# Attention of a hybrid backbone in two parts: the first latent tile ahead of the other three

## The reference

```python
h = x * (1 + scale1) + shift1                       # one combined input projection h @ w_in
o_rec = hgrn2_branch(...)                           # 8 heads, gated linear recurrence, both directions
o_att = attend(q, k, v)                             # 16 query heads of 64, 4 key heads, 640 keys for latent tokens
y = sigmoid(ga) * (o_rec @ w_branch_rec) + sigmoid(gb) * (o_att @ w_branch_att)
x = layer_norm(ALPHA * x + g1 * (y @ w_out))
h2 = x * (1 + scale2) + shift2
# PEER mixer: 8 heads, two top-16 lists of 128 keys each, then the top 16 of 16*16 sums
s = einsum(h2 @ w_query, sub_keys); s_top, i_top = top_k(s, 16)
best_s, best_pos = top_k(s_top[0][:, None] + s_top[1][None, :], 16); gate = softmax(best_s)
a = gelu(einsum(h2, u_tab[expert]))                 # 128 experts for each token, a row of 1024 each
x = layer_norm(ALPHA * x + g2 * einsum(gate * a, v_tab[expert]))
```

## Time and profile before

| what | value |
|---|---|
| median of 3 runs | 5783.16 us (5782.72 to 5789.52) |
| the profiled execution | 5785.87 us, span 5783.8 us |
| PE busy | 4596.6 us (79%) |
| DVE busy | 3766.0 us (65%) |
| POOL busy | 2196.6 us (38%) |
| ACT busy | 1375.0 us (24%) |
| moved by DMA | 1705.85 MB, mean 295 GB/s |

### The profile page before, as it was taken

One profiled execution on the slowest core, in us unless ns is written; L12 is line 12 of the kernel. 1 busy time (PEld: TensorE's weight loads), 2 busy tenths in 40 slices (PEclk: granted clock), 3 DMA queues, 4 the chain that ended last, 5 costly groups with the idle time before them and its releaser, 6 DMA issues. The chain is left out here.

```text
span 5783.8 us, 60711 instructions
## 1 busy us (share of the span) xinstructions
PE 4596.6 (79%) x17704; PEld 2562.3 (44%) x17704; DVE 3766.0 (65%) x7088; ACT 1375.0 (24%) x3576; POOL 2196.6 (38%) x1826
## 2 busy tenths in 40 slices
PE   7889988876856877777788999988778678777776
PEld 6556655644523332222265566556454343222222
DVE  2356778767788776754533477787677887667545
ACT  2112212310001333333321122122110013333333
POOL 0001124442656444455400011344416564444554
PEclk9899998888978999999999999978889789999999
DMA  6743345685979999999967433456959899999998
GB/s 262 264 179 104 120 150 206 209 334 219 354 295 377 381 421 420 416 421 416 398 220 269 148 113 125 177 188 205 347 198 377 303 349 392 421 421 415 420 415 346
DMA packets 296660, 1705.85 MB, mean 295 GB/s; under 512 B 33424, under 2 KB 43280, under 8 KB 176272
## 3 DMA queue, kind: packets, MB, share of 16 engines
q0 software_dynamic: 258048, 1342.29, 59.6%
q1 hardware_dynamic: 23712, 338.18, 15.4%
q10 hardware_dynamic: 14576, 21.52, 1.0%
HBM read 1696.61 MB, written 5.24 MB: 294 GB/s over the span
## 5 line engine op out<-in xcount | busy, mean ns | idle before, releaser
L366 POOL DMA_INDIRECT arena<-in_peer_uv,eidx x1024 | 1179.5, 1152 | 1642.3 <-POOLq L365 1402.0
L2148 DVE SCALAR_TENSOR_TENSOR arena<-arena 128x1024 f32<-128x1024 f32 x384 | 470.6, 1225 | 353.8 <-DMA arena<-in_peer_uv,eidx 342.7
L409 POOL DMA_INDIRECT arena<-in_peer_uv,eidx x384 | 504.0, 1313 | 477.8 <-POOLq L408 455.0
L864 PE MATMUL banks<-arena 128*128 128x512 f32 x896 | 493.3, 633 | 234.8 <-PEq L1476 231.5
L837 PE MATMUL banks<-ring,arena 128*128 128x512 f32 x864 | 386.7, 603 | 115.9 <-PEq L819 115.1
L866 PE MATMUL banks<-arena 128*128 128x512 f32 x896 | 469.8, 606 | 0.0
L461 ACT ACTIVATE arena<-arena 128x1 f32<-128x1 f32 (+1 forms) x772 | 156.9, 203 | 1044.7 <-ACTq L460 1044.5
L864 PEld LDWEIGHTS banks<-arena 128*128 128x128 f32 x896 | 151.5, 194 | 546.7 <-issue 546.4
L466 ACT ACTIVATE arena<-ident,arena 128x128 f32<-128x128 f32 x832 | 333.6, 401 | 238.3 <-ACTq L465 235.8
L2148 DVE SCALAR_TENSOR_TENSOR ring<-ring,arena 128x1024 f32<-128x1024 f32 x192 | 235.3, 1226 | 216.6 <-DMA ring<-in_peer_uv,eidx 214.3
L1879 DVE SCALAR_TENSOR_TENSOR arena<-arena 128x1024 f32<-128x1024 f32 x256 | 328.3, 1282 | 67.4 <-DMA arena<-in_peer_uv,eidx 50.7
(11 more groups left out here) (303 smaller groups left out, 7858.6 us busy)
## 6 DMA issues: line engine op xcount, KB each, us to landing
ring<-in_wblk SPq DMA_DIRECT2D x160, 2048.0 KB
arena<-in_peer_uv,eidx POOLq DMA_INDIRECT x1408
arena<-in_lnrows ACTq DMA_DIRECT2D x6, 1024.0 KB, 10.3
arena<-in_sk ACTq DMA_DIRECT2D x4, 1024.0 KB, 8.2
hT<-in_peer_uv,eidx POOLq DMA_INDIRECT x192
ring<-in_peer_uv,eidx POOLq DMA_INDIRECT x192
x<-in_x_sample ACTq DMA_DIRECT2D x1, 2048.0 KB, 28.9
out<-arena ACTq DMA_DIRECT2D x4, 512.0 KB, 7.3
```

The source lines that it names most:

```text
L366: nc.gpsimd.indirect_dma_start(grow[j], None, ins["peer_uv"], bass.IndirectOffsetOnAxis(ap=eidx[:, n, r:r + 1].bitcast(U32), axis=0)).then ...
L409: nc.gpsimd.indirect_dma_start(gslot[j], None, ins["peer_uv"].rearrange("(e h) d -> e (h d)", h=2), bass.IndirectOffsetOnAxis(ap=eidx[:, n ...
L864: nc.tensor.matmul(banks[:, b, :], diag[n], row[:, 0:CB], start=start, stop=stop, skip_group_check=True).then_inc(diag_used, 1)
L2148: V.scalar_tensor_tensor(u, u, 1.0, h2[:, t - 2, :], ALU.mult, ALU.mult, accum_out=av[:, r:r + 1])
```

## The change

Attention is split in two. First come two groups of eight units that hold all 16 heads of tile 1 (`LONE`, `members`), then tile 1's mixing, norm, queries and scores, then eight groups of six units for tiles 2 to 4. Tile 1's selection leaves `one_mix` and becomes 16 parts (`select_block`), one after each of the first 16 units of the second attention; from the 18th unit on two dots of tile 1 follow each unit, 60 in all. The mixing steps of tiles 2 to 4 then take 15 rows each (68 dots, then sums), and the rest of the 96 sums comes where all of them were.

Tile 0's rows move forward: 24 dots ahead of the first recurrence head (`GATE_ROWS`), 13 in each head, 44 sums among the norms, 32 in the first attention, 52 in tile 1's mixing (10 of them behind it). Tile 1's buffers now lie where row slots 4 to 7 are, so from sum 76 on tile 0's rows use four slots (`NARROW`), and tile 1's rows from the fifth on wait for the end of its selection (`slots_open`). The gelu of tile 0 moves to the start of the key stage.

Tiles 2 to 4 get buffers of their own (`grp_tile`), with a second load of the norm rows and sub-keys and a second spread of the modulation rows (`gains_in`, `fold_gains`). The selection of tile 2 starts by blocks as its scores come, and gives its row numbers in two halves (`joined_ids`). The second norm of tile 0 is finished between tile 2's rows. The queries are transposed straight from `qkv`, without POOL's copy.

```diff
-HEAD_ROWS = 6
-NORM_ROWS = 24
+GATE_ROWS = 24
+HEAD_ROWS = 13
+NORM_ROWS = 44
 UNIT_ROWS = 2
+NARROW = 76
+ONE_UNIT = 18
+ONE_EXP = 20
+ONE_ROWS = 2
+MIX_ROWS = 15
+
+
+def members(g):
+
+    if g < LONE:
+        return [(4 * g + n, 1) for n in range(4)]
+    return [(g - LONE, t) for t in range(2, NT)]
+
+
+def units_of(g):
+
+    return 2 * len(members(g))
...
 
+        def row_slot(part, r):
+
+            return r % 4 if part == 1 and r >= NARROW else r % ROWS
...
+        one_jobs = ONE_ROWS * (2 * GT * PAIRS - ONE_UNIT)
+        gelu_mix = (SLOTS - one_jobs + MIX_ROWS - 1) // MIX_ROWS + 1
+        assert one_jobs <= SLOTS and gelu_mix < KD
...
+                n, first, last = part % 2, 0, SLOTS
                 for r in range(first, last):
-                    j = r % ROWS
+                    j = row_slot(part, r)
                     if n == 0 and r % (SLOTS // 2) == 0:
                         stage_rows(r)
+                    if part == 2 and r == 4:
+                        pool.wait_ge(slots_open, 1)
+                        pool.sem_inc(slots_open, -1)
...
             for l in range(DEPTH):
-                ahead = dots_end + ROWS
-                single_rows(0, 0, min(ahead, SLOTS))
-                for p in range(PAIRS):
-                    if p in (0, PAIRS // 2):
-                        pool.wait_ge(qkn_pool, 1)
-                        pool.sem_inc(qkn_pool, -1)
-                    stage_queries(p)
-                    if p:
-                        for r in range(ahead, ahead + UNIT_ROWS * UNITS):
-                            if r < 2 * SLOTS:
-                                single_rows(r // SLOTS, r % SLOTS, r % SLOTS + 1)
-                        ahead += UNIT_ROWS * UNITS
-                for r in range(ahead, 2 * SLOTS):
-                    single_rows(r // SLOTS, r % SLOTS, r % SLOTS + 1)
-                single_rows(0, 0, SLOTS)
-                single_rows(1, 0, SLOTS)
+                for part in range(4):
+                    single_rows(part)
                 for t in range(2, NT):
                     n = t % 2
...
+                        if r in ((0, SLOTS // 2) if t == 2 else (0,)):
+                            c = slice(r, r + SLOTS // 2 if t == 2 else SLOTS)
+                            pool.wait_ge(idx_ready, 1)
+                            pool.sem_inc(idx_ready, -1)
+                            nc.gpsimd.tensor_copy(eidx[:, n, c].bitcast(U32), eid[:, 0, c].bitcast(U32)
+                                                  ).then_inc(idx_staged, 1)
+                            pool.wait_ge(idx_staged, 1)
+                            pool.sem_inc(idx_staged, -1)
+                            if c.stop == SLOTS:
+                                pool.sem_inc(idx_taken, 1)
...
 
+                gelu(0, SLOTS).then_inc(gelu_ready, 1)
                 act.dma_start(kpast, ins["cache_k"][l:l + 1].rearrange("a p n -> p (a n)")).then_inc(past_full, 16)
...
+                def attention(first, last):
+                    for b in (0, 2, 6):
+                        claim_pair(b)
+                    queries(first)
+                    claim(4)
+                    pe.sem_inc(bank_free[4], 1)
+                    for u in range(2):
+                        score(first, u)
+                    for g in range(first, last):
+                        att_group(g, g == first, g < last - 1)
+                    weigh(last - 1, units_of(last - 1) - 1)
+                    output(last - 1)
+                    for b in (0, 2, 6):
+                        pe.sem_inc(bank_free[b], 1)
+
+                attention(0, LONE)
                 phase_barrier(pe, "pe")
-
-
                 one_first = len(CTX_BLOCKS + LAT_BLOCKS)
                 one_mix(one_tile, one_first)
+                attention(LONE, GROUPS)
+                phase_barrier(pe, "pe")
+
+
                 grp_first = one_first + len(ONE_BLOCKS)
...
+                def joined_ids(half):
+
+                    c = slice(half * SLOTS // 2, (half + 1) * SLOTS // 2)
+                    V.scalar_tensor_tensor(e1[:, c], e1[:, c], float(NKEYS), e2[:, c], ALU.mult, ALU.add)
+                    dve.drain()
+                    if half == 0:
+                        dve.wait_ge(idx_taken, 1)
+                        dve.sem_inc(idx_taken, -1)
+                    V.tensor_scalar(eid[:, 0, c].bitcast(U32), e1[:, c], layer_base[:], None, ALU.add
+                                    ).then_inc(idx_ready, 1)
+
...
-                            ctx_rows((2 * SLOTS - jobs["at"] + 3 - n) // (4 - n))
+                            ctx_rows((2 * SLOTS - jobs["at"] + 4 - n) // (5 - n))
+                    fold_gains(tl)
...
+                def select_block(tl, n, part):
+
+                    if part == 0:
                         if n < 2:
                             dve.wait_ge(stage_ready, 1)
                             dve.sem_inc(stage_ready, -1)
-                        first_level(tl, tl.stage, 4 * n, 4 * n + 4)
+                        first_level(tl, tl.stage, 4 * n, 4 * n + 2)
+                    if part == 1:
+                        first_level(tl, tl.stage, 4 * n + 2, 4 * n + 4)
+                    if part == 2:
                         candidates(tl, 2 * n, 2 * n + 2)
                         second_level(tl, 2 * n, 2 * n + 2)
+                    if part == 3:
                         positions(gates[0], 2 * n, 2 * n + 2)
                         look_up_both(tl, 2 * n)
                         if n == 1:
                             dve.wait_ge(stage_ready, 2)
                             dve.sem_inc(stage_ready, -2)
                             one_ids(0)
+                        if n == 3:
+                            one_ids(1)
...
+                ctx_rows(GATE_ROWS)
+                softmax(gates[0])
...
+                def att_group(g, first, more):
+                    n = units_of(g)
+                    for u in range(n):
                         if u % 2:
                             arrived(4)
                             V.tensor_copy(PT[1], r3(pair(4, KEYS), P)).then_inc(bank_free[4], 1)
                             dve.drain().then_inc(pt_ready[1], 1)
-                        if u + 2 < UNITS:
-                            lowest(b, u + 2)
+                        if u + 2 < n:
+                            lowest(g, u + 2)
                         elif more:
-                            lowest(1 - b, u + 2 - UNITS)
-                        if u == 0 and p:
-                            normalise(1 - b)
-                        if u < 7 and p == 0:
-                            head_norm(512, 8, P, u)
-                        if u == 6 and p == 0:
-                            dve.drain().then_inc(qkn_pool, 1)
-                        ctx_rows(rows_at_unit(p, u))
-
-                for u in range(2):
-                    lowest(0, u)
-                for p in range(PAIRS):
-                    att_pair(p)
-                normalise(1)
+                            lowest(g + 1, u + 2 - n)
+                        if u == 0 and not first:
+                            normalise(g - 1)
+                        if g == 0 and u < 2:
+                            for part in ((2, 3), (4, 5, 6))[u]:
+                                head_norm(512, 8, P, part)
+                            if u == 1:
+                                dve.drain().then_inc(qn_ready, 1)
+                        if g < LONE:
+                            ctx_rows(UNIT_ROWS)
+                        else:
+                            at = (g - LONE) * n + u
+                            if at < 16:
+                                select_block(one_tile, at // 4, at % 4)
+                                if at == 15:
+                                    dve.drain().then_inc(slots_open, 1)
+                            if at >= ONE_UNIT:
+                                one_dots(ONE_ROWS * (at - ONE_UNIT), ONE_ROWS * (at - ONE_UNIT + 1))
+                            if at == ONE_EXP + 3:
+                                softmax(gates[0])
+
+                def attention(first, last):
+                    for u in range(2):
+                        lowest(first, u)
+                    for g in range(first, last):
+                        att_group(g, g == first, g < last - 1)
+                    normalise(last - 1)
+
+                for part in range(2):
+                    head_norm(512, 8, P, part)
+                attention(0, LONE)
                 phase_barrier(dve, "dve")
                 one_mix(one_tile)
+                ctx_rows(2 * SLOTS - jobs["at"])
+                dve.wait_ge(g2_ready, 1)
+                dve.sem_inc(g2_ready, -1)
+                second_norm(0, acc, bc2c, None, 0)
+                attention(LONE, GROUPS)
+                phase_barrier(dve, "dve")
 
...
-                mix(0)
-                for n in range(1, KD):
+                own = {"at": one_jobs}
+                for n in range(KD):
                     mix(n)
```

(66 more changed lines are left out.)

360 lines of the change are left out of this document (161 added, 199 removed).

## The result

The changed kernel took 5857.94 us (median of 4 runs, 5849.4 to 5865.5), the kernel before 5782.94 in the same comparison: a ratio of 1.0127, 95% interval 1.011 to 1.0145. It is slower by 75 us, where I forecast a gain of 58. The time lies outside my range and has the other sign.

A forecast was written before the change was run, and what follows sets the result against it. No engine bound the whole kernel; each stage had its own bound (DVE and PE in the heads, DMA in mixing). The terms summed to -29 us a layer, -58 in both: 5725 against the median of 5783.16, range 5635 to 5805.

The forecast's parts named there:

- The heads: Recurrence heads: seven more dots lie inside the chain of levels, 8.05 us a head, +64 us a layer.
- The lead-in: Ahead of the heads: 24 dots fit into DVE's wait and PE's wait mostly goes, -5 us a layer (0 to -9).
- The key stage: Key stage: sums, norms, gelu and waits take 94 us against 69, +25 a layer, bounds +15 and +32.
- Attention: Both attention parts: 99 and 245 us, together 344 against 317, +27 a layer, bounds +15 and +45.
- Tile 1's mixing: Tile 1's mixing and what follows: fewer rows, -32, and less behind it, -16; together -48 us a layer, bounds -70 and -15.
- Four slots: Rival in tile 1's mixing: four slots are too few, a row costs about 3 us, -48 becomes -11, 5799 us; chance 0.12.
- The sign that I had named: Tile 1's mixing: if no shorter than 132 us to its last row, the prediction is wrong.
- The mixing of tiles 2 to 4: Mixing of tiles 2 to 4: DVE is free when it begins, DMA is next in line, -50 us a layer, bounds -60 and -35.
- The end: From the last mixing step to tile 2's rows: PE's 44.92 us wait goes, -42 us a layer, bounds -50 and -25.
- The clock in the heads: Rival in the heads: PE pauses, its clock falls to 1.2 GHz, some 264 us a layer beyond the +64; chance 0.10.
- The heads hide their rows: Rival in the heads: DVE's idle time hides the dots, +20 for +64 a layer, 5637 us; chance 0.10.
- the end wins nothing: Rival ahead of tile 2's rows: query blocks starve the 51 sums, so these rows start no sooner, 5809 us; chance 0.08.

The follow-up runs named there:

- the four-slot run: The kernel before with tile 0's rows going through four slots, not eight, from sum 68 on, nothing else moved: 5863.62 us, ratio 1.0136.
- two of its versions: The kernel before, unedited (5782.94 us), and with 24 dots while gates are made and five of six dots a head behind its levels (5710.25 us).
- its last version: The changed kernel with eight rows before each mixing, five dots a head behind the levels and two under ACT's square root: 5631.58 us, ratio 0.9743.

## Why the prediction was wrong, step by step

- **The heads** (+64): right, with the mechanism. Seven dots are 8.05 us a head; with the lead-in it was +65. The level is 5.00 us long in the trace (592.52 to 597.52), 4.9 was forecast. The lead-in won nothing (-5): the first head starts on DVE at 458 in both kernels, since the last of the 24 dots ends at 456.3, where the softmax had stood. DVE did ten dots without a pause and then waited for the eleventh row:

```profile
438.46 1.23 DVE L1911 SCALAR_TENSOR_TENSOR arena<-arena 128x1024 f32<-128x1024 f32 x1 [6.76 <-DMA arena<-in_peer_uv,eidx]
```

Of the 16 issues that I had priced at the slow or the fast rate, four took 1.98 to 1.99 us, all beside dots without a gap between them, and ten 0.93 to 0.98 us: five while DVE waited, five beside dots that stood about 0.1 us apart. So the slow rate that my rule from the Trainium skill ("SBUF — State Buffer", Who interferes with whom) gave for all 16 held for a quarter of them. Two of the four lie on the way of the eleventh row, some 2 of the 6.76 us by this estimate; the rest is the way of the rows themselves, and from 438.4 on they came at 407 GB/s with DMA full.
- **The key stage** (+25): +33. The sums, the norms and the gelu were priced well. DVE stood 5.28 us ahead of the gelu's first reader, but 3.45 us stood at this place before, where the engines meet (`phase_barrier`); from PE's start behind the barrier (892.41) to the first sum (895.97) it was 3.6 us, and I had given 3. What I had too low were the waits: those for rows came to 7.4 us for 4 to 5, and 3 us stand at the norms, for which I had no term. The changed kernel, and then the kernel before:

```profile
894.17 0.29 DVE L1906 TENSOR_TENSOR arena<-arena 128x128 f32<-128x128 f32 x1 [5.28 <-DVEq L1905]
```

```profile
827.31 1.23 DVE L1876 SCALAR_TENSOR_TENSOR arena<-arena 128x1024 f32<-128x1024 f32 x1 [3.45 <-DVEq L295]
```

- **Attention** (+27): +29. 97 and 249 us for 99 and 245; selection in the units was priced rightly. One thing I had not reckoned with: PE took 266.6 us for the matmuls of both parts, at a mean clock of 0.75 and 0.80, where it had taken 251.8 at 0.83. Whether this lengthened attention isn't shown.
- **Tile 1's mixing** (-48): the step that failed, -6 in the trace. From attention's end to y it was 108 us for 111 where I had -32, behind it -7 for -16; PE's queries +4. Two causes can be told apart, and by the runs both have a size. *Rows with eight slots* cost 1.6 us in the part up to y (27 rows in 82.3, 45 in 110.9). So 13 rows fewer are worth 21, not 32: my lower bound of 17 was the better value. Of what I added to it, the 10 us of waits for weights were time in which rows came anyway, and the last 5 us have no term in the prediction at all. *Four slots:* the same line gives 90 us for 32 rows, and the trace has 108: 18 us, and about 9 behind y, if ten rows cost there as the 15 of the four-slot run did (13). That is some 26 us a layer, 52 in both, as an estimate between runs; the four-slot run, with 60 rows, showed 64 to 86 by itself. I had this rival, at +37 a layer, and gave it 0.12, because "fewer rows in flight make the queue that they wait in shorter". This is the sentence that failed. A row's way does get shorter, but not by half: under the weight blocks eight slots at 2.2 us a row are at most 18 us from issue to issue of a slot, four at 2.8 are 11. So fewer rows come, first because the weight blocks take a larger part of a full DMA, and then, behind the last block, because four rows in flight leave DMA idle (282 GB/s and a share of 0.82 in the changed kernel from 1169 to 1195, 406 and 1.02 in the kernel before). The sign that I had named, 132 us to the stage's last row, stood at 131.7; it was 130.3 in the kernel before, so it could tell little.
- **The mixing of tiles 2 to 4** (-50): -40. "DMA is next in line" was wrong by a stretch. It was DVE, which began 20 us late and took the rows of a step ahead of its y; PE stood 19.34 us for it. Rows taken in those first 20 us gave the missing time back, 21 us.
- **The end** (-42): -38. PE's wait of 44.92 us is gone as forecast. Waits of PE of 13.31, 3.09 and 2.99 us came into its queries and scores, where one of 4.77 had been; I had left them as they were. The longest is no wait for weights: the two blocks that it could have waited for had come in by 1782, and the next was asked for only at 1822.42. The profile names nothing for it:

```profile
1822.68 12.13 PE L1470 MATMUL banks<-hT,ring 128*128 128x384 f32 x32 [13.31 <-issue]
```

- The clock in the heads was 0.97, with DVE the longer of the chain: that rival is out, and the rule of the Trainium skill beside it ("TensorE: Matmul & The Clock Gate", A second HAM failure mode) doesn't show in this stage. *The heads hide their rows* and *the end wins nothing* are out too.

By layer the deviation is 72 us: 42 from tile 1's mixing, 10 from the mixing of tiles 2 to 4, 8 from the key stage, 6 from heads and lead-in, 4 from the end, 2 from attention. Of the 42, some 26 are the four slots and 12 the price of a row; 4 are PE's queries. Even the rival's own time, 5799, is 59 us short of the measured one, since it left the other steps as forecast.

What stays open: the changed kernel with eight slots was not tried, since its buffers for tile 1 lie in the other four. Its cost is taken from the kernel before, by the line through two of its versions. What holds PE in the query matmuls of tiles 2 to 4, some 15 us a layer in the changed kernel and nothing in its last version, isn't shown either.

## What to carry to other kernels

When an edit takes staging buffers from a stream of gathers that shares DMA with a stream of weights, price a gather anew: here it was 2.4 us with four in flight and 2.0 with eight, in the same kernel and with the same 45 rows. Ask of each piece of filler work not how long it is but which wait it stands in: the same five dots cost 5.7 us a head inside the chain of levels and nothing behind it. Where an engine stands idle at the head of a stage with its data present, and the stage ends with that engine, start its filler ahead of the first step; then look for the engine that is longest once the filler is gone, since a gain stops there (43 us a head).

## What the runs showed of the hardware

- With eight row transfers in flight beside the weight blocks the stage ran at 395 GB/s and a share of 0.98; with four at 336 and 0.89 in the changed kernel, and 2.7 us a row for 2.0. In the kernel before with nothing but four slots, DMA stayed full while weight blocks came (401 GB/s, share 1.00); four transfers of 0.52 MB in flight alone gave 262 GB/s and 0.80.
- An issue of a row by POOL (422 to 457 in the changed kernel) took 1.98 to 1.99 us four times, beside dots that followed each other without a gap, and 0.93 to 0.99 us nearly everywhere else, also beside dots that stood about 0.1 us apart.
- In attention the granted clock rose from 0.87 to 0.97 when DVE's part of a unit became shorter and PE went from 79% busy to 86%. The same 1094 matmuls took 183 us for 203. So a shorter filler on DVE came with shorter matmuls on PE, and the gain was larger than the work taken away.
